# Two of the four last parts of the next item's token gather moved behind the scatter, in each expert item

## The chip, the cores and the metric

The kernel runs on one core of one Trainium2 chip. The metric is the device time of one launch in microseconds (us), lower is better. PE is TensorE's matmul, PEld its weight load, DVE VectorE, ACT ScalarE, SP the engine that starts the weight transfers. A matmul in float32 leaves two MATMUL and two LDWEIGHTS records in the trace, so a group of 4 matmuls reads x8.

## What is computed

Two decoder layers on 256 tokens of 1024 values, everything in float32. Each layer is a mixer (three attention patterns in one, a forgetting attention, an output projection), a layer norm, a mixture of 16 experts, and a second layer norm. The change lies in the expert part:

```python
def expert_block(args):
    xblk, e = args                      # tokens routed to expert e
    a = jax.nn.silu(xblk @ w_gate[e]) * (xblk @ w_up[e])
    return a @ w_down[e]                # three 1024 x 1024 float32 matrices each
...
out = jnp.zeros((T + 1, D)).at[row_tok].add(yb * row_gate[:, None])[:T]
...
h = layer_norm(DEEPNORM_ALPHA * h + y, ln2_g[l], ln2_b[l])
```

Every token goes to two experts of one group, and the two results are weighed by its gates.

## The kernel before

Both layers run as a hardware loop of two turns on every engine. In a layer the attention and the router come first. Then a second hardware loop (L874 on PE, its like on ACT and DVE) runs over the layer's **items**: an item is one expert with up to 32 tokens (tiny), 64 (narrow) or 128 (wide), and the kind of each item is worked out on the chip and read into registers. In the profiled execution there are 24 tiny, 9 narrow and 1 wide item in all, 16 or more per layer. The code of the three kinds lies in three branches, and those of tiny, narrow and wide items each have a part for experts of even and one for experts of odd number.

What an item does on PE, in program order:

- wait for `xg_ready` (the item's tokens, gathered and copied to SBUF as `xg`), then take the branch by kind and by odd or even;
- the gate and the up product (`quarter` L592 for tiny, `halves` L580 for narrow, `wide_product` L687 for wide), with weights that stream through `ring`;
- `gather` (L567) for the next item, parts 0 to 3. A gather is a matmul with a 0/1 matrix `place_t` made by DVE; part k brings 128 of the 1024 values of each token, so the eight parts fill two banks of `lo`, and the semaphore `gathered` counts up after part 3 and after part 7;
- the turning of the activations, then the down product into `lo`;
- gather, parts 4 to 7;
- the scatter (L645 in `scatter_halves`, L727 in the wide item), a matmul that adds the item's result `y` to the layer's sum in `acc`. It waits for `y_ready`.

DVE has its own fixed order for an item: `place_gates` (L1180) for this item and `place_tokens` (L1173) for the next, the product of gate and up, the copy of the turned gates, `copy_gathered(turn, 0)`, then the copy of the down product to `y` (L1390 tiny, L1399 narrow, L1409 wide; it ends in `y_ready`), then `copy_gathered(turn, 1)`. The latter (L1187) waits for `gathered` after part 7, copies the second bank to `xg` and raises `xg_ready`. After the last item DVE waits for `scattered` and starts the second layer norm (L1062). The last item of a layer gathers for an item that doesn't exist, and DVE copies that too.

SP streams each expert's gate, up and down matrices, 4 MB each in two transfers of 2 MB, into `ring`: gate and up have two homes (even and odd experts), down has one. In program order it waits for the gate of item e to be read (`gate_half`, `gate_done`), loads the gate of e + 2, does the same with up, then waits for down of e and loads down of e + 1 (L347).

The tail of an item before the change:

```python
pe.wait_ge(placeT_ready, g + 1)
gather(range(4, KB))
scatter_halves(g)
```

Of the kernel before, what the change touches and what calls it, by code (L numbers as in the profile page):

```python
# [43 lines left out]
KB = D // P  # L44
# [114 lines left out]
def build(nc, x, w_in, w_out, w_gate, w_up, w_down, small, router, ln, consts, out):  # L159
    with ExitStack() as ctx:  # L160
# [277 lines left out]
        def _(pe):  # L438
# [123 lines left out]
            def gather(ks, release=None):  # L562

                for k in ks:
                    for t in range(TB):
                        mm = nc.tensor.matmul(lo[:, 2 + k // 4, (k % 4) * P:(k % 4 + 1) * P],  # L567
                                              h[:, t, k * P:(k + 1) * P], place_t[:, t],
                                              start=(k % 4 == 0 and t == 0), stop=(t == 1), skip_group_check=True)
                        if release is not None and k == ks[0] and t == 0:  # L570
                            mm.then_inc(release, 1)
                    if k % 4 == 3:
                        mm.then_inc(gathered, 1)

            def halves(bank, lhsT, s, kk, start, stop):

                for half in range(2):
                    at = kk * D + half * 512
                    mm = nc.tensor.matmul(lo[half * W:(half + 1) * W, bank, :], lhsT, ring[:, s, at:at + 512],  # L580
                                          start=start, stop=stop, skip_group_check=True)
                return mm

            def turn_gates():

                for t in range(TB):
                    mm = nc.tensor.transpose(lo[:, 3, t * P:(t + 1) * P], place_tg[:, t], ident)
                mm.then_inc(placeT_done, 1)

            def quarter(at, bank, lhsT, s, col, start, stop):  # L590

                return nc.tensor.matmul(lo[at * T:(at + 1) * T, bank, :], lhsT, ring[:, s, col:col + 512],  # L592
                                        start=start, stop=stop, skip_group_check=True)
# [19 lines left out]
            def tiny_item(full, g, turn):  # L613

                pe.wait_ge(place_ready, turn + 1)
                gather(range(3))
                pe.wait_ge(act_ready, g + 1)
                turn_gates()
                for b in range(4):
                    mm = nc.tensor.transpose(lo[:, 1, b * W:(b + 1) * W], act[0:W, b * P:(b + 1) * P], ident[0:W, 0:W])  # L620
                mm.then_inc(act_turned, 1)
                gather(range(3, 4))
                pe.wait_ge(act_t_ready, g + 1)
                for s in range(4):
                    if s % AT_ONCE == 0:
                        pe.wait_ge(ring_full[DOWN + s], full)
                    for half in range(2):
                        for kk in range(2):
                            f = 2 * s + kk
                            at = (f % 4) * W + (f // 4) * T  # L630
                            mm = quarter(2 * half + kk, 0, act_t[:, at:at + T], DOWN + s, kk * D + half * 512,
                                         s == 0, s == 3)
                    if s % AT_ONCE:
                        mm.then_inc((down_half, down_done)[s // AT_ONCE], 1)
                pe.wait_ge(placeT_ready, g + 1)
                gather(range(4, KB))
                scatter_halves(g)

            def scatter_halves(g):

                pe.wait_ge(y_ready, g + 1)
                for t in range(TB):
                    for half in range(2):
                        r = slice(half * W, (half + 1) * W)
                        mm = nc.tensor.matmul(acc[:, 2 * t + half, :], place_gt[r, t * P:(t + 1) * P], y[r, 0:512],  # L645
                                              start=False, stop=True, skip_group_check=True)
                mm.then_inc(scattered, 1)
# [12 lines left out]
            def narrow_item(full, g, turn):  # L660

                pe.wait_ge(place_ready, turn + 1)
                gather(range(3))
                pe.wait_ge(act_ready, g + 1)
                for b in range(4):
                    mm = nc.tensor.transpose(lo[:, 1, b * P:(b + 1) * P], act[:, b * P:(b + 1) * P], ident)
                mm.then_inc(act_turned, 1)
                turn_gates()
                gather(range(3, 4))
                pe.wait_ge(act_t_ready, g + 1)  # L670
                for s in range(4):
                    if s % AT_ONCE == 0:
                        pe.wait_ge(ring_full[DOWN + s], full)
                    for kk in range(2):
                        f = 2 * s + kk
                        at = (f % 4) * P + (f // 4) * W
                        mm = halves(0, act_t[:, at:at + W], DOWN + s, kk, f == 0, f == KB - 1)
                    if s % AT_ONCE:
                        mm.then_inc((down_half, down_done)[s // AT_ONCE], 1)
                pe.wait_ge(placeT_ready, g + 1)  # L680
                gather(range(4, KB))
                scatter_halves(g)

            def wide_product(bank, lhsT, s, kk, start, stop):
                for half in range(2):
                    at = kk * D + half * 512
                    mm = nc.tensor.matmul(lo[:, bank + half, :], lhsT, ring[:, s, at:at + 512],  # L687
                                          start=start, stop=stop, skip_group_check=True)
                return mm
# [12 lines left out]
            def wide_item(full, g, turn):  # L702

                pe.wait_ge(act_ready, g + 1)
                for b in range(KB):
                    mm = nc.tensor.transpose(lo[:, b // 4, (b % 4) * P:(b % 4 + 1) * P], act[:, b * P:(b + 1) * P],
                                             ident)
                mm.then_inc(act_turned, 1)
                turn_gates()  # L710
                pe.wait_ge(place_ready, turn + 1)
                gather(range(4))
                pe.wait_ge(act_t_ready, g + 1)
                for s in range(4):
                    if s % AT_ONCE == 0:
                        pe.wait_ge(ring_full[DOWN + s], full)
                    for kk in range(2):
                        f = 2 * s + kk
                        mm = wide_product(0, act_t[:, f * P:(f + 1) * P], DOWN + s, kk, f == 0, f == KB - 1)
                    if s % AT_ONCE:  # L720
                        mm.then_inc((down_half, down_done)[s // AT_ONCE], 1)
                pe.wait_ge(placeT_ready, g + 1)
                gather(range(4, KB))
                pe.wait_ge(y_ready, g + 1)
                for t in range(TB):
                    for half in range(2):
                        mm = nc.tensor.matmul(acc[:, 2 * t + half, :], place_gt[:, t * P:(t + 1) * P],  # L727
                                              y[:, half * 512:(half + 1) * 512],
                                              start=False, stop=True, skip_group_check=True)
                mm.then_inc(scattered, 1)  # L730

            def turn_raw(t, banks, release=None):

                for b in range(2):
                    for i in range(4):
                        k = 4 * b + i
                        mm = nc.tensor.transpose(banks[b][:, i * P:(i + 1) * P], raw[:, t, k * P:(k + 1) * P], ident)
                        if release is not None and k == 0:
                            mm.then_inc(release, 1)
                    mm.then_inc(turned, 1)  # L740
# [45 lines left out]
            with pe.Fori(0, DEPTH) as l:  # L786
# [87 lines left out]
                with pe.Fori(0, n) as j:  # L874
# [10 lines left out]
                    with pe.If(kind < TINY_KINDS):  # L885
                        with pe.If(odd < 1):
                            tiny_gate_up(EVEN, UP, even_full, even_full)
                        with pe.Else():
                            tiny_gate_up(ODD, ODD_UP, odd_full, odd_up_full)
                        tiny_item(full, g, turn)  # L890
# [545 lines left out]
```

## Time and profile before

| | us |
|---|---|
| three runs | 1303.62, 1308.72, 1309.84 (median 1308.72) |
| the profiled execution | 1304.05 |
| its span, first to last instruction | 1302.4 |
| PE busy in it | 1094.1 (84%) |
| DVE busy | 351.2 (27%) |
| ACT busy | 184.8 (14%) |
| weights and the rest read from HBM | 443.11 MB, mean 341 GB/s over the span |

The profile cuts the span into 40 slices of 32.6 us. The expert items of the first layer run from about 174 to 613 us, those of the second from about 793 to 1289 us; the rest is attention and router. Busy shares are means over these stages, so each stage is read by itself, from the chain of waits, the DMA's share in short stretches, and the timeline around one item's end.

### The profile page before, as it was taken

How to read it: one execution, taken by the hardware profiler on the slowest of the kernel's cores; microseconds unless marked ns; L12 is line 12 of the kernel's file. 1: busy time of each engine (PE TensorE's matmuls, PEld its weight loads, DVE VectorE, ACT ScalarE, POOL GpSimd, SP SyncE). 2: the span in 40 equal slices, each digit the busy share in tenths (PEclk: the TensorE clock that was granted, in tenths of full speed). 3: DMA queues.
4: the chain of work that ended last, by engine and by line, in shares of the span. 5: the costliest groups of instructions: out<-in, count | busy, mean ns of one | idle time of the engine just before them, and what ended most of it. 6: DMA issues, size and time to landing. Idle time of an engine off the chain costs nothing.

```text
span 1302.4 us, 17517 instructions
## 1 busy us (share of the span) xinstructions
PE 1094.1 (84%) x6296; PEld 550.1 (42%) x6297; DVE 351.2 (27%) x853; ACT 184.8 (14%) x375; POOL 4.6 (0%) x12
## 2 busy tenths in 40 slices
PE   7999979799966779777999997898998876776585
PEld 5676543344422333323676653343443432232232
DVE  0764650011111111113366463111011111111123
ACT  2233310000010000010223321001001000010000
POOL 0000000000000000000000000000000000000000
PEclk9999998899987789889899998899999988787898
DMA  9914389999999999999931542359989999999994
GB/s 376 384 65 187 130 368 428 389 428 428 429 430 428 428 428 430 429 408 422 391 130 65 194 184 108 154 233 405 429 333 421 430 427 429 428 429 429 427 406 193
DMA packets 34712, 444.71 MB, mean 341 GB/s; under 512 B 4080, under 2 KB 4336, under 8 KB 5872
## 3 DMA queue, kind: packets, MB, share of 16 engines
q1 hardware_dynamic: 33520, 439.97, 80.9%
q0 software_dynamic: 1152, 4.19, 0.8%
q8 instruction: 26, 0.43, 0.1%
q14 instruction: 14, 0.11, 0.0%
HBM read 443.11 MB, written 1.05 MB: 341 GB/s over the span
## 4 chain that ended last, share of the span: by engine, by line
PE 55%; DMA 37%; issue 4%; DVE 3%; ACT 0%; DVEq 0%; ACTq 0%; SPq 0%
DMA ring<-in_w_down_dram 37%; PE lo L580 12%; PE acc L491 9%; PE lo L592 8%; PE acc L469 5%; PE lo L567 5%; PE lo L687 3%; PE acc L555 3%; PE acc L645 2%; PE lo L555 1%; PE acc L533 1%; PE lo L521 1%; PE lo L510 1%; PE acc L754 1%; PE lo L508 1%
## 5 line engine op out<-in xcount | busy, mean ns | idle before, releaser
L592 PE MATMUL lo<-ring,work 128*32 128x512 f32 x2304 | 297.5, 664 | 140.9 <-DMA ring<-in_w_down_dram 125.8
L592 PEld LDWEIGHTS lo<-ring,work 128*32 128x32 f32 x2304 | 78.3, 117 | 336.9 <-issue 172.5
L580 PE MATMUL lo<-ring,work 128*64 128x512 f32 x864 | 196.4, 611 | 28.4 <-issue 21.6
L567 PEld LDWEIGHTS lo<-work,h 128*128 128x128 f32 x1152 | 138.1, 193 | 64.2 <-issue 59.2
L567 PE MATMUL lo<-work,h 128*128 128x128 f32 x1152 | 156.8, 285 | 3.7 <-DVE work L1311 1.9
L580 PEld LDWEIGHTS lo<-ring,work 128*64 128x64 f32 x864 | 63.3, 141 | 154.1 <-issue 146.2
L491 PE MATMUL acc<-ring 128*128 128x256 f32 x512 | 119.2, 388 | 0.0
L491 PEld LDWEIGHTS acc<-ring 128*128 128x128 f32 x512 | 98.4, 195 | 20.0 <-issue 7.4
L1026 ACT ACTIVATE work<-lo 64x512 f32<-64x512 f32 x24 | 14.3, 594 | 488.2 <-PE lo L592 488.2
L1390 DVE COPY work<-lo 128x512 f32<-128x512 f32 x24 | 16.6, 692 | 231.2 <-PE lo L592 231.2
L469 PE MATMUL acc<-ring 128*128 128x512 f32 x128 | 62.5, 633 | 3.8 <-ACT ring L924 3.8
L645 PE MATMUL acc<-work 64*128 64x512 f32 x264 | 65.6, 615 | 0.0
L1187 DVE COPY work<-lo 128x512 f32<-128x512 f32 x68 | 47.0, 692 | 59.8 <-PE lo L567 59.6
L1385 DVE TENSOR_TENSOR work<-lo,work 64x512 f32<-64x512 f32 x24 | 16.4, 682 | 140.3 <-ACT work L1026 140.3
L687 PE MATMUL lo<-ring,work 128*128 128x512 f32 x96 | 41.6, 593 | 0.6 <-issue 0.6
L555 PE MATMUL acc<-ring,work 128*128 128x512 f32 x88 | 41.7, 603 | 0.0
L1394 DVE TENSOR_TENSOR work<-lo,work 128x512 f32<-128x512 f32 x9 | 6.2, 692 | 127.2 <-PE lo L580 127.2
L469 PEld LDWEIGHTS acc<-ring 128*128 128x128 f32 x128 | 24.6, 202 | 31.3 <-issue 30.0
L1180 DVE TENSOR_SCALAR work<-cst,rank_tab,gate_tab 128x128 f32 x68 | 20.5, 344 | 60.1 <-issue 60.1
L1137 DVE TENSOR_TENSOR work<-work,cst 32x512 f32<-32x512 f32 x48 | 32.8, 683 | 13.0 <-ACT work L937 11.5
L1026 ACT ACT_TABLE_LOAD x24 | 30.8, 1283 | 21.9 <-issue 21.9
L645 PEld LDWEIGHTS acc<-work 64*128 64x128 f32 x264 | 22.7, 186 | 19.5 <-issue 15.5
(190 smaller groups left out, 658.5 us busy)
## 6 DMA issues: line engine op xcount, KB each, us to landing
ring<-in_w_gate_dram SPq DMA_DIRECT2D x64, 2048.0 KB, 18.4
ring<-in_w_up_dram SPq DMA_DIRECT2D x64, 2048.0 KB, 24.2
ring<-in_w_down_dram SPq DMA_DIRECT2D x64, 2048.0 KB, 23.8
ring<-in_w_in_dram SPq DMA_DIRECT2D x24, 1024.0 KB, 26.2
ring<-in_w_out_dram SPq DMA_DIRECT2D x8, 1024.0 KB, 29.0
ln_gb<-in_ln_dram POOLq DMA_DIRECT2D x8, 512.0 KB, 11.4
cst<-in_consts_dram SPq DMA_DIRECT2D x1, 1420.0 KB, 17.5
h<-in_x_dram SPq DMA_DIRECT2D x1, 1024.0 KB, 5.2
```

The lines of the kernel that those rows point to most:

```text
L469: mm = nc.tensor.matmul(acc[:, 3 if u else 1, :], actT[:, k, t * P:(t + 1) * P], ring[:, s, (k % 4) * CH:(k % 4 + 1) * CH], start=(k == 0) ...
L491: mm = nc.tensor.matmul(acc[:, 1, i * SEQ:(i + 1) * SEQ], ring[:, s, at:at + P], actT[:, k, :], start=(k == 0 and i == 0), stop=(k == KB - ...
L555: mm = nc.tensor.matmul(banks[half], oT[:, k, t * P:(t + 1) * P], wout[:, k, half * 512:(half + 1) * 512], start=(k == first), stop=(k == ...
L567: mm = nc.tensor.matmul(lo[:, 2 + k // 4, (k % 4) * P:(k % 4 + 1) * P], h[:, t, k * P:(k + 1) * P], place_t[:, t], start=(k % 4 == 0 and t ...
L580: mm = nc.tensor.matmul(lo[half * W:(half + 1) * W, bank, :], lhsT, ring[:, s, at:at + 512], start=start, stop=stop, skip_group_check=True)
L592: return nc.tensor.matmul(lo[at * T:(at + 1) * T, bank, :], lhsT, ring[:, s, col:col + 512], start=start, stop=stop, skip_group_check=True)
L645: mm = nc.tensor.matmul(acc[:, 2 * t + half, :], place_gt[r, t * P:(t + 1) * P], y[r, 0:512], start=False, stop=True, skip_group_check=True)
L687: mm = nc.tensor.matmul(lo[:, bank + half, :], lhsT, ring[:, s, at:at + 512], start=start, stop=stop, skip_group_check=True)
L1026: nc.scalar.activation(silu[0:W, 0:512], lo[W:P, 0, :], ACT.Silu).then_inc(silu_done, 1)
L1137: nc.vector.tensor_tensor(turned_part[to], raw[at], sin[at], ALU.mult)
L1180: nc.vector.tensor_scalar(place_tg[:, t], places[:, bass.ds(kind * P, P)], rank_tab[:, t, bass.ds(expert, 1)], gate_tab[:, t, bass.ds(expe ...
L1187: op = nc.vector.tensor_copy(xg[:, 4 * half:4 * half + 4, :], lo[:, 2 + half, :].rearrange("p (k s) -> p k s", k=4))
```

## The change

In the three kinds of item the second half of the gather is cut in two: parts 4 and 5 stay ahead of the scatter, parts 6 and 7 are issued after it. No instruction is added or taken away, and neither DVE's, ACT's nor SP's program changes. The semaphore `gathered`, which counts up after part 7, so comes after the scatter. Line numbers behind the edits move by one to three.

```diff
@@ tiny_item (and narrow_item, word for word the same)
                 pe.wait_ge(placeT_ready, g + 1)
-                gather(range(4, KB))
+                gather(range(4, 6))
                 scatter_halves(g)
+                gather(range(6, KB))
@@ wide_item
                 pe.wait_ge(placeT_ready, g + 1)
-                gather(range(4, KB))
+                gather(range(4, 6))
                 pe.wait_ge(y_ready, g + 1)
                 for t in range(TB):
                     for half in range(2):
...
                 mm.then_inc(scattered, 1)
+                gather(range(6, KB))
```

PE, the end of a tiny item (L592 down product, L567 gather, L645 and then L646 scatter), before:

```order
L592 MATMUL lo<-ring,work 32x512 [waits ring_full10]
L592 MATMUL lo<-ring,work 32x512 x7
L567 MATMUL lo<-work,h 128x128 [waits placeT_ready]
L567 MATMUL lo<-work,h 128x128 x7
L645 MATMUL acc<-work 128x512 [waits y_ready]
L645 MATMUL acc<-work 128x512 x3
L885 UNCONDITIONAL_BRANCH
```

and with the change:

```order
L592 MATMUL lo<-ring,work 32x512 [waits ring_full10]
L592 MATMUL lo<-ring,work 32x512 x7
L567 MATMUL lo<-work,h 128x128 [waits placeT_ready]
L567 MATMUL lo<-work,h 128x128 x3
L646 MATMUL acc<-work 128x512 [waits y_ready]
L646 MATMUL acc<-work 128x512 x3
L567 MATMUL lo<-work,h 128x128 x4
L888 UNCONDITIONAL_BRANCH
```

Four of the eight gather matmuls (two parts of two matmuls each) went from ahead of the scatter to behind it; they are now the last work of the item on PE.

PE, the end of the wide item (L687, then L689, the down product; L727, then L729, the scatter), before:

```order
L687 MATMUL lo<-ring,work 128x512 x7
L567 MATMUL lo<-work,h 128x128 [waits placeT_ready]
L567 MATMUL lo<-work,h 128x128 x7
L727 MATMUL acc<-work 128x512 [waits y_ready]
L727 MATMUL acc<-work 128x512 x3
```

and with the change:

```order
L689 MATMUL lo<-ring,work 128x512 x7
L567 MATMUL lo<-work,h 128x128 [waits placeT_ready]
L567 MATMUL lo<-work,h 128x128 x3
L729 MATMUL acc<-work 128x512 [waits y_ready]
L729 MATMUL acc<-work 128x512 x3
L567 MATMUL lo<-work,h 128x128 x4
```

The same move, with a scatter of four full-height matmuls. DVE's order stays as it was. From the copy of `y` in a narrow item over the end of the loop to the second layer norm it reads, in the kernel before:

```order
L1399 COPY work<-lo 128x512 [waits down_done]
...
L1187 COPY work<-lo 128x512 [waits gathered]
L1392 UNCONDITIONAL_BRANCH
L1373 REGISTER_ALU
L1373 COMPARE_AND_BRANCH
L1412 REGISTER_ALU
L1062 BN_STATS stats<-acc 128x6 [waits scattered]
```

Nothing moved here: the copy that waits for `gathered` stands ahead of the layer norm that waits for `scattered`, before and after.

## Rows read from the trace of the kernel before

**Rows 1.** The page: the chain that ended last; GB/s in 40 slices.

```profile
PE 55%; DMA 37%; issue 4%; DVE 3%; ACT 0%; DVEq 0%; ACTq 0%; SPq 0%
GB/s 376 384 65 187 130 368 428 389 428 428 429 430 428 428 428 430 429 408 422 391 130 65 194 184 108 154 233 405 429 333 421 430 427 429 428 429 429 427 406 193
```

**Rows 2.** Stretches: us, busy PE, PEld, DVE, ACT, POOL; PEclk, DMA share, GB/s.

```profile
238.00:242.00 4.00, 4.00 (x22) 1.41 (x20) 0.00 (x0) 0.00 (x0) 0.00 (x0) 0.98 0.65 197
242.00:300.00 58.00, 56.95 (x296) 24.55 (x294) 8.56 (x18) 4.93 (x6) 0.00 (x0) 1.00 0.99 422
...
864.00:880.00 16.00, 15.52 (x100) 6.34 (x104) 3.16 (x7) 1.28 (x1) 0.00 (x0) 1.00 0.01 4
...
973.00:977.00 4.00, 4.00 (x42) 1.18 (x37) 0.00 (x0) 0.00 (x0) 0.00 (x0) 1.00 0.36 70
977.00:1240.00 263.00, 191.93 (x1328) 81.28 (x1324) 40.22 (x84) 22.72 (x30) 0.00 (x0) 0.87 1.00 428
```

**Rows 3.** Timeline of SP, the weight transfers: start us, us, engine, line, what.

```profile
240.59 3.69 SPq L347 DMA_DIRECT2D ring<-in_w_gate_dram  x2
...
268.76 3.69 SPq L347 DMA_DIRECT2D ring<-in_w_gate_dram  x2
...
296.79 3.69 SPq L347 DMA_DIRECT2D ring<-in_w_gate_dram  x2
...
879.35 3.69 SPq L347 DMA_DIRECT2D ring<-in_w_gate_dram  x2
...
975.28 3.69 SPq L347 DMA_DIRECT2D ring<-in_w_gate_dram  x2
```

**Rows 4.** Timeline, a tiny item's end and the next one's start.

```profile
1244.26 2.05 PE L567 MATMUL lo<-work,h 128*128 128x128 f32 x16
...
1244.40 0.69 DVE L1390 COPY work<-lo 128x512 f32<-128x512 f32 x1 [14.32 <-PE lo L592]
...
1246.25 1.99 PE L645 MATMUL acc<-work 64*128 64x512 f32 x8
1246.35 0.69 DVE L1187 COPY work<-lo 128x512 f32<-128x512 f32 x1 [1.26 <-PE lo L567]
...
1248.38 0.19 PEld L592 LDWEIGHTS lo<-ring,work 128*32 128x32 f32 x8 [0.97 <-issue]
1248.41 7.07 PE L592 MATMUL lo<-ring,work 128*32 128x512 f32 x64 [0.17 <-issue]
```

**Rows 5.** Timeline, the scatter between two narrow items.

```profile
290.57 1.99 PE L645 MATMUL acc<-work 64*128 64x512 f32 x8
...
292.88 13.96 PE L580 MATMUL lo<-ring,work 128*64 128x512 f32 x64 [0.32 <-issue]
```

**Rows 6.** Timeline, layer one's first item: the copy to xg, then the gate.

```profile
172.60 1.07 ACT L1016 COPY work<-lo 128x512 f32<-128x512 f32 x2 [10.60 <-PE lo L567]
...
174.36 0.19 PEld L592 LDWEIGHTS lo<-ring,work 128*32 128x32 f32 x8 [1.98 <-issue]
...
174.39 7.07 PE L592 MATMUL lo<-ring,work 128*32 128x512 f32 x64 [1.82 <-ACT work L1016]
```

**Rows 7.** Timeline, the end of the wide item and the tiny one behind it.

```profile
966.28 1.29 DVE L1409 COPY work<-lo 128x512 f32<-128x512 f32 x2 [13.04 <-PE lo L687]
...
967.86 3.60 PE L727 MATMUL acc<-work 128*128 128x512 f32 x8
...
971.39 0.16 PEld L592 LDWEIGHTS lo<-ring,work 128*32 128x32 f32 x8 [0.76 <-issue]
```

**Rows 8.** Timeline, the end of the second layer's items.

```profile
1287.17 0.69 DVE L1187 COPY work<-lo 128x512 f32<-128x512 f32 x1 [1.26 <-PE lo L567]
...
1289.10 1.29 DVE L1062 BATCH_NORM_STATS2 stats<-acc 128x6 f32<-128x512 f32 x2 [1.24 <-PE acc L645]
```

**Rows 9.** Timeline of PE, gate and up products behind longer gaps.

```profile
235.29 7.19 PE L580 MATMUL lo<-ring,work 128*64 128x512 f32 x26 [6.41 <-issue]
...
826.60 9.76 PE L592 MATMUL lo<-ring,work 128*32 128x512 f32 x64 [3.44 <-issue]
```

More of the change, by code:

```diff
@@ L722, in wide_item @@
                 pe.wait_ge(placeT_ready, g + 1)
-                gather(range(4, KB))
+                gather(range(4, 6))
                 pe.wait_ge(y_ready, g + 1)
@@ L730, in wide_item @@
                 mm.then_inc(scattered, 1)
+                gather(range(6, KB))
             def turn_raw(t, banks, release=None):
```

## The prediction

> **What bounds the kernel now.** I read the chain first. It is PE for 55% of the span and DMA for 37% [rows 1], so neither is the bound throughout, and the question is where each holds. The GB/s slices answer roughly: some 428 GB/s through most of both expert stages, far less at the start of the second one (108, 154, 233, then 333 once more, [rows 1]). Short stretches then say where the DMA runs dry. In the first layer it has a hole at 238 to 242 us and is full from there [rows 2]. In the second it stands still from 864 to 880, is low once more at 973 to 977, and is then full for 263 us at 428 GB/s [rows 2]. Each hole ends with SP issuing a gate transfer, at 240.59, 879.35 and 975.28 [rows 3]; SP had waited for PE to read the gate of an item. So up to such a point the time belongs to PE, and whatever makes PE later there moves the whole transfer stream behind it. Behind it, the stream sets the time, and a PE that is a microsecond later only waits a microsecond less for its next down matrix. The very end of each layer, after the last down half has landed, is PE's and DVE's again.
>
> The item's end is next. In a tiny one the second gather starts at 1244.26 and the scatter at 1246.25, while DVE copies y from 1244.40 to 1245.09 [rows 4]. y is therefore there 1.1 us before PE gets to the scatter. DVE then copies xg, 1246.35 to 1247.04, under the scatter, and the next gate's weights are loaded at 1248.38 [rows 4]. The scatter hides the copy completely. The gap behind it is 0.17 us here and 0.32 us in a narrow item [rows 4, 5].
>
> **What the change does at an item's end.** PE's work stays the same: 2.0 us of gather and 2.0 us of scatter. The gather ahead of the scatter shrinks to half, 1.0 us, against a copy of y that is ready 0.83 us after the gather's start (1245.09 less 1244.26). That wait stays hidden, with 0.2 us to spare; I allow 0.05 us for a later first weight load. So nothing is won: PE did not wait for y before. What is lost is the cover of the xg copy. `gathered` now comes with the last matmul of the item, about 1248.3. DVE starts 0.11 us after PE has finished the gather (as 1246.35 follows the gather's end at 1246.24), copies for 0.69, and is done near 1249.1. From there to the next gate's weight load I need a row in which PE waits at exactly that place: the first item of the layer. There the copies end at 172.60 + 1.07 = 173.67 and the weights load at 174.36, 0.69 us later [rows 6]; two branches lie in between. Sum: 1249.1 + 0.69 = 1249.8, against 1248.38. **An open boundary costs 1.4 us.** Its bounds: with nothing between copy and load it is 0.7; with the whole 1.34 us that lie between 1247.04 and 1248.38 it is 2.05.
>
> Which value holds turns on what the 1.34 us are. Either PE's sequencer was already waiting at `xg_ready` and the path from there really takes 1.34, or it came later, held up by reading two register values for the loop. I take 0.69, because in [rows 6] the wait for the copy is certainly the last. The page "TensorE: Matmul & The Clock Gate" of the Trainium skill (its table of specs) gives TensorE's queue a depth of 64, which would let the sequencer run past an item's 32 tail instructions and stand at the wait early; by that rule the boundary would cost 2.05 us and the total near 19. No row here shows the depth, and [rows 6] has the shorter path; the case is the first rival below.
>
> The wide item is different. Its copy of y takes two instructions and ends at 966.28 + 1.29 = 967.57, some 0.5 us later than a half gather from 966.08 or so would end, so PE waits for y and the scatter starts near 967.65 instead of 967.86. Its first gate load behind came at 971.39, with no gap [rows 7]. Now: scatter to 971.3, gather to 972.3, copy 972.4 to 973.1, gate at 973.8. **The wide boundary costs 2.4 us** (1.7 to 3.1).
>
> **Which boundaries count.** First layer: the hole closes at 240.59, when item 2 has read its first gate half; it began at 235.29 [rows 9]. Ahead of it lie the boundaries 0 to 1 and 1 to 2, both with the change's gap in full: 2 x 1.4 = 2.8. Behind it the DMA is full, but barely: a narrow item takes PE 296.79 - 268.76 = 28.0 us [rows 3], and its six transfers of 2.1 MB at 428 GB/s take 29.4. With 1.4 more PE needs 29.4 as well. The gate issue at 268.76 comes about 3 us before the six transfers from 240.59 are through (first data some 1.9 us after the issue, then 29.4), and with the same 1.9 us of latency the margin is 1.2 us. The boundary 2 to 3 eats 1.4 of it, and the next ones hold it level. I put **0.5** for this (0 to 1.5). Items behind 350 us are tiny, their PE work is a fraction of 29.4, and nothing of the change is seen.
>
> Second layer: 879.35 is the gate of item 3, behind the boundaries 0 to 1, 1 to 2 and 2 to 3. Boundary 3 to 4 is hidden, item 4 waits for its down matrix. Items 4 to 5 (into the wide one) and 5 to 6 (out of it) lead to 975.28. That is 4 x 1.4 + 2.4 = **8.0**. All boundaries behind 977 are hidden under the 263 us of full DMA [rows 2].
>
> **The two layer ends.** One could expect a gain of 1 us here, since the scatter ends a microsecond earlier. But DVE's copy of xg stands ahead of the layer norm in its program. Today that copy is done at 1287.86 and DVE idles 1.24 us until the scatter ends [rows 8]. Now the copy waits for part 7, behind the scatter. All PE work still ends at about 1289.05, just ahead of today's statistics, DVE copies 1289.16 to 1289.85, and the statistics follow at once, as DVE's instructions queue back to back: 1289.9 against 1289.10. **0.8 us each**, 1.6 in all, between 0.7 and 2.0 each (if leaving the loop on DVE took the 1.24 us that it now has free). The first layer's end reads alike, and the next layer's PE work waits for it.
>
> **Sum:** 2.8 + 0.5 + 8.0 + 1.6 = **12.9 us**. The profiled execution becomes 1304.05 + 12.9 = 1317.0. The three runs lie at 1303.6 and at 1308.7 to 1309.8, so I add to the middle, 1306.5, and say 1319.5.
>
> **Rivals.**
>
> *The longer path.* 1.34 us from xg to gate at every boundary: 6 x 2.05 + 3.1, and narrow items of 30.1 us against 29.4 of DMA, which cost 2 instead of 0.5; with 1.6 for the ends +19.0, or 1325.5. For it: the row of 1248.38. Against: [rows 6].
>
> *The clock falls in the new gaps.* Behind 3.44 us of idle the gate and up products of a tiny item took 9.76 us instead of 7.07, at a granted clock of half (1.2 GHz) at first [rows 4, 9]. The new gaps are near 1.5 us; the first item's gate came after 1.82 us of idle and still took 7.07 [rows 6]. If two or three of the seven boundaries pay 2.7 each, +6.5: about 1326.
>
> *Code loading swallows part of it.* Three of the seven boundaries have a stall that nothing in the profile explains, two of over 6 us and one of 3.44 (two of the three in [rows 9]), each at the first visit of a branch, so I take them for the loading of code. If that starts before the wait for xg, it runs beside it and three times 1.4 fall away: +8.7, 1315.
>
> *The other side: the clock comes back sooner.* Four gate phases start at half clock behind a stall (the two of [rows 9] among them) and lose up to 2.7 us each (9.76 less 7.07), 10.8 together at most, on the path that counts. Where the clock rises depends on when the work starts. If a start 1 to 3 us later cut all four to nothing, and the boundaries cost only 0.7 each, the sum would be 6 x 0.7 + 1.7 + 1.6 - 10.8 = -3.3, 1303. It decides from the point at which these phases run in 7.1 (tiny) and 14.0 us (narrow) right away. Nothing in the trace speaks for it except that the loss is there to be regained.
>
> **How the numbers follow.** Forecast 0.62, longer path 0.13, clock falls 0.10, code loading 0.10, clock back sooner 0.05. The range takes in the first four: low 1303.6 + (6 x 0.7 + 1.7 + 2 x 0.7) = 1311 by the lower bounds, high 1309.8 + 19.4 = 1329, rounded up by half a microsecond. A difference of under 0.5%, 6.5 us, can't be told from none. The forecast is twice that. Of the forecast's own 0.62 I give 0.03 to ending under 6.5, of the code loading case 0.05 more, of the last rival 0.02 to a gain and 0.03 to none: slower 0.87, same 0.11, faster 0.02.
>
> **What would show it.** In the profile after: y copied before PE gets to the scatter in tiny and narrow items, and a wait of 0.5 us for y in the wide one; PE idle 1.5 us ahead of each gate product, put down to DVE's copy L1190, which starts 0.1 us behind part 7; the SP issue of 240.59 near 243.4, that of 879.35 some 8 later (3.3 of the first layer, 0.8 of its end, 4.2), that of 975.28 some 12 later; the full stream of 263 us as long as before; the first statistics of a layer right behind an xg copy. It is wrong if the gaps stay near 0.3 us, if the DMA shows no hole where I count PE, or if the statistics start ahead of the xg copy.

## The result and the profile after

The change makes the kernel slower by 0.95% (ratio 1.0095, 95% interval 1.0078 to 1.0112), or about 12.4 us (10.2 to 14.6). The median is 1318.32 us against 1304.14 us, 7 runs each, so the medians lie 14.2 us apart; the 12.4 us are the ratio's. 1319.5 had been forecast. The profiled execution of the changed kernel took 1320.83 us, at a span of 1319.1, so it lies at the slow end of its own runs (1314.41 to 1321.48).

| | before, us | after, us |
|---|---|---|
| median | 1304.14 | 1318.32 |
| span of the profiled execution | 1302.4 | 1319.1 |
| PE busy | 1094.1 | 1105.9 |
| DVE busy | 351.2 | 351.0 |

Both kernels issue 17517 instructions. PE's busy time grew by 11.8 us with the same matmuls: 11.0 of it are the gather's (156.8 to 167.8), mostly because two halves of a gather read 1.16 us each in these records, and a whole one 2.05. The page of the changed kernel, the chain and GB/s in 40 slices (as [rows 1]):

```profile
PE 59%; DMA 32%; issue 5%; DVE 4%; DVEq 0%; ACT 0%; ACTq 0%; SPq 0%
GB/s 377 374 65 192 152 372 426 360 403 427 426 427 429 429 429 428 429 408 422 338 128 84 172 237 52 212 171 409 427 309 401 427 428 428 429 428 429 429 399 176
```

PE's share of the chain rose from 55 to 59% and the DMA's fell from 37 to 32%: the stretch in which the stream of weights sets the time starts later, it isn't slower (the rows from 992 us on, below). The groups of waits say what PE and DVE now wait for (who waited for whom: us, times, longest):

```profile
DVE work L1190 <- PE lo L567: 134.5, 59, 4.7
...
PE lo L592 <- DVE work L1190: 32.1, 21, 1.6
```

In the kernel before, DVE waited 59.6 us for the gather, and PE had no wait of this kind on DVE among its large ones. Now 21 gate products of tiny items wait for DVE's copy to xg, 1.5 us each. That is the new wait. A boundary is the end of one item and the start of the next. Here is one in full, between the same two tiny items as in [rows 4]. Timeline of the changed kernel, with start, duration, engine, line, tile, and in brackets the idle time before:

```profile
1262.29 1.99 PE L646 MATMUL acc<-work 64*128 64x512 f32 x8
...
1264.20 1.16 PE L567 MATMUL lo<-work,h 128*128 128x128 f32 x8
1265.40 0.69 DVE L1190 COPY work<-lo 128x512 f32<-128x512 f32 x1 [3.83 <-PE lo L567]
1266.76 0.19 PEld L592 LDWEIGHTS lo<-ring,work 128*32 128x32 f32 x8 [1.59 <-issue]
1266.79 1.49 PE L592 MATMUL lo<-ring,work 128*32 128x512 f32 x12 [1.43 <-DVE work L1190]
```

The scatter now comes first, then parts 6 and 7. DVE starts its copy when they are done and ends at 1266.09; PE loads the next gate's weights at 1266.76, 0.67 us later. Nothing of PE's work covers this: it idles for 1.43 us, where it had idled for 0.17.

The trace also holds the records of PE's sequencer, the part that reads the program and feeds the array, and they say where the 1.34 us between copy and gate went in [rows 4]. There the sequencer leaves the item's branch at 1245.17, loads its two register values from 1246.19 on (TENSOR_LOAD, 0.3 us each) and comes to the wait for `xg_ready` at 1247.64, 0.6 us after the copy's end at 1247.04. In the changed kernel it is there at 1264.84 and stands until 1266.13, just behind the copy's end. The same holds at every boundary without a long stall, in two traces of each kernel: before, the sequencer comes 0.5 to 1.2 us after the copy; with the change it comes 1.2 to 1.4 us ahead of the copy's end, 3.0 behind the wide item.

To see which of the 34 boundaries count, I cut both kernels at the same events. Each number is the time between two rows of a timeline; both kernels were profiled a second time, unedited (below), so there are two looks at each. "Issue of item n" is the first SP gate transfer behind the start of that item's gate product, and item 0 is a layer's first.

| stretch | before | after | forecast |
|---|---|---|---|
| start to item 0's second gather | 188.24, 189.44 | 187.97, 188.66 | 0 |
| to the issue of item 2 (240.59 in [rows 3]) | 52.35, 52.08 | 54.44, 54.82 | +2.8 |
| to the last item's second gather | 368.59, 369.20 | 371.16, 370.99 | +0.5 |
| to the statistics | 4.02, 4.02 | 4.81, 4.81 | +0.8 |
| to layer 2, item 0's second gather | 205.99, 206.26 | 206.89, 207.31 | 0 |
| to the issue of item 3 | 60.16, 60.24 | 65.09, 65.04 | +4.2 |
| to the issue of item 6 | 95.93, 95.94 | 99.52, 99.55 | +3.8 |
| to the last item's second gather | 309.80, 309.71 | 311.21, 309.58 | 0 |
| to the statistics | 4.02, 4.02 | 4.81, 4.81 | +0.8 |

The map holds where it can be tested. In the eighth row lie eleven boundaries, each with its 1.5 us gap, and the stretch reads 309.6 and 311.2 us; the kernels of the experiments read 309.7 to 309.8 or 311.0 to 311.7 there, and late_before, with the gather's order untouched, 311.2. So the change costs nothing in it. The sixth and seventh rows hold six boundaries and gain 8.5.

Two looks don't carry the first layer's rows. The two kernels of the experiments that keep the gather's order and the time (late_before, act_late_before) read 54.1 and 54.3 us in the second row and 370.9 and 370.7 in the third, as much as the changed kernel or nearly so. Of the 2.4 us that the second row gained, 1.2 are its two boundaries; the rest is two products behind long stalls, which run at half clock at first in every trace and together took 33.2 us on the mean in place of 31.9. In the fifth row, where I forecast nothing, the two looks gain 1.0, and all fourteen traces spread over 204.2 to 208.1.

The DMA's holes and the full stretch behind them, in the changed kernel (columns as in [rows 2]):

```profile
864.00:890.00 26.00, 24.27 (x148) 10.72 (x148) 4.28 (x9) 2.47 (x3) 0.00 (x0) 1.00 0.26 109
...
988.00:992.00 4.00, 4.00 (x40) 1.42 (x36) 0.48 (x2) 0.00 (x0) 0.00 (x0) 1.00 0.35 74
992.00:1256.00 264.00, 195.94 (x1328) 82.46 (x1320) 40.23 (x84) 22.72 (x30) 0.00 (x0) 0.88 1.00 428
```

From 992 the stream runs full for 264 us at 428 GB/s, as it did from 977.

### The profile page after: what moved, and what is told of

It is laid out like the page before. It is cut to its first block, busy times and chain, and to the rows that moved or that the text cites. A ratio compares the mean times of both kernels' runs of the same rounds, so it can differ in the third digit from the quotient of the medians.

```text
span 1319.1 us, 17517 instructions
## 1 busy us (share of the span) xinstructions
PE 1105.9 (84%) x6296; PEld 556.0 (42%) x6297; DVE 351.0 (27%) x853; ACT 184.8 (14%) x375; POOL 4.6 (0%) x12
## 4 chain that ended last, share of the span: by engine, by line
PE 59%; DMA 32%; issue 5%; DVE 4%; DVEq 0%; ACT 0%; ACTq 0%; SPq 0%
DMA ring<-in_w_down_dram 32%; PE lo L580 15%; PE lo L592 9%; PE acc L491 9%; PE lo L567 6%; PE acc L469 5%; PE lo L689 3%; PE acc L555 3%; PE acc L646 2%; PE lo L555 1%; PE acc L533 1%; PE lo L521 1%; DVE work L1190 1%; PE lo L510 1%; PE acc L757 1%
## 5 line engine op out<-in xcount | busy, mean ns | idle before, releaser
L592 PE MATMUL lo<-ring,work 128*32 128x512 f32 x2304 | 296.6, 662 | 141.4 <-DMA ring<-in_w_down_dram 101.6
L580 PE MATMUL lo<-ring,work 128*64 128x512 f32 x864 | 200.5, 622 | 30.9 <-issue 26.5
L592 PEld LDWEIGHTS lo<-ring,work 128*32 128x32 f32 x2304 | 78.4, 117 | 317.7 <-issue 185.9
L567 PEld LDWEIGHTS lo<-work,h 128*128 128x128 f32 x1152 | 142.8, 195 | 92.8 <-issue 87.8
L567 PE MATMUL lo<-work,h 128*128 128x128 f32 x1152 | 167.8, 291 | 3.0 <-DVE work L1314 1.9
L646 PE MATMUL acc<-work 64*128 64x512 f32 x264 | 65.6, 615 | 0.0
L1388 DVE TENSOR_TENSOR work<-lo,work 64x512 f32<-64x512 f32 x24 | 16.4, 683 | 116.2 <-ACT work L1029 116.2
L689 PE MATMUL lo<-ring,work 128*128 128x512 f32 x96 | 41.6, 593 | 1.9 <-issue 1.9
L469 PEld LDWEIGHTS acc<-ring 128*128 128x128 f32 x128 | 24.9, 203 | 31.9 <-issue 30.6
L1140 DVE TENSOR_TENSOR work<-work,cst 32x512 f32<-32x512 f32 x48 | 32.8, 683 | 12.4 <-ACT work L940 11.0
L646 PEld LDWEIGHTS acc<-work 64*128 64x128 f32 x264 | 22.7, 186 | 19.6 <-issue 15.8
## 6 DMA issues: line engine op xcount, KB each, us to landing
ring<-in_w_gate_dram SPq DMA_DIRECT2D x64, 2048.0 KB, 17.5
```

The lines of the kernel that those rows point to most:

```text
L469: mm = nc.tensor.matmul(acc[:, 3 if u else 1, :], actT[:, k, t * P:(t + 1) * P], ring[:, s, (k % 4) * CH:(k % 4 + 1) * CH], start=(k == 0) ...
L1140: nc.vector.tensor_tensor(turned_part[to], raw[at], sin[at], ALU.mult)
```

## The experiments

All kernels were timed against the kernel before on the same chips; a ratio is followed by its 95% interval.

### Is it the copy to xg, and does it matter how much is moved?

One part behind the scatter in place of two:

```diff
-                gather(range(4, 6))
+                gather(range(4, 7))
...
-                gather(range(6, KB))
+                gather(range(7, KB))
```

> Only part 7 of the gather stands behind the scatter, parts 4 to 6 ahead. Theory (the cost of a boundary is the copy to xg that no PE work covers any more, plus the 0.7 us from there to the next gate): it doesn't matter how many parts stand behind, as long as the last one does. Gaps of 1.4 to 1.8 us ahead of the gate as with the change, statistics at a layer's end right behind the copy, and the time of the changed kernel, +0.9 to +1.1% over before (about +12 us). Rival (the cost grows with what is moved, such as each switch between scatter and gather matmuls): half of it, about +6 us, gaps near 0.9 us.

Measured: 1.0098 (1.0074 to 1.0122), +12.8 us. The time from an item's second gather to the next gate is the same as with two parts behind to 0.1 us: 5.75 against 5.75 us at the second narrow-to-narrow boundary, 5.64 against 5.64 at a tiny one, 4.81 at both layer ends. Only behind the wide item it is shorter, 7.16 against 7.60, because three parts ahead of the scatter hide y's copy but for 0.04 us. Half the move costs the whole price. What counts is that the last part, and with it `gathered`, stands behind the scatter.

All four parts behind the scatter:

```diff
-                gather(range(4, 6))
                 scatter_halves(g)
-                gather(range(6, KB))
+                gather(range(4, KB))
```

> All four parts stand behind the scatter, none ahead. Theory: the cover of DVE's copy of y is gone too. The y copy is ready some 0.9 us behind the last down matmul, so PE idles about 0.9 us ahead of each scatter (1.5 in the wide item) and again 1.5 us ahead of the gate. A boundary costs 2.4 us in place of 1.5, a layer's end 1.7 in place of 0.8, and a narrow item takes PE about 30.4 us against 29.3 of DMA. Sum near +21 us, +1.6% over before. Rival (the wait for y is hidden in the queue, only the copy to xg counts): as with the change, +12 us.

Measured: 1.0212 (1.0191 to 1.0234), +27.7 us, more than the 21 expected. The two waits stand in the trace one behind the other. Timeline of four_parts, a narrow item's end:

```profile
297.20 0.69 DVE L1399 COPY work<-lo 128x512 f32<-128x512 f32 x1 [6.54 <-PE lo L580]
298.01 0.33 PEld L645 LDWEIGHTS acc<-work 64*128 64x128 f32 x4 [1.73 <-issue]
298.04 1.99 PE L645 MATMUL acc<-work 64*128 64x512 f32 x8 [0.88 <-DVE work L1399]
...
299.96 2.05 PE L567 MATMUL lo<-work,h 128*128 128x128 f32 x16
302.05 0.69 DVE L1187 COPY work<-lo 128x512 f32<-128x512 f32 x1 [4.15 <-PE lo L567]
303.59 0.20 PEld L580 LDWEIGHTS lo<-ring,work 128*64 128x64 f32 x4 [1.77 <-issue]
303.59 1.94 PE L580 MATMUL lo<-ring,work 128*64 128x512 f32 x8 [1.58 <-DVE work L1187]
```

PE idles 0.88 us for y ahead of the scatter, as forecast, and 1.58 us for xg ahead of the gate. So the two parts that the change leaves ahead of the scatter are what hides y. Where the other 7 us are: the narrow items now follow each other at 30.4 us against 29.4 of transfers, and the stretch from item 2's issue to the layer's last gather grew to 373.4 us, as it did in one_part and only_narrow; the one from item 3's to item 6's issue grew by 8.3, where the expected prices make 5.7 (2.4 for a boundary, and 2.4 + 0.9 for the wide one). I didn't take it further apart, so this part stays open.

### Give the copy its cover back

PE waits for xg's second bank only where the gate product first reads it, at part 4; the first bank gets a semaphore of its own. The same edit on the changed kernel (late_after) and on the kernel before (late_before):

```diff
@@ narrow_matrix, gate only (and tiny_gate_up, wide_matrix)
                     if i % AT_ONCE == 0:
                         pe.wait_ge(ring_full[first + i], full)
+                    if i == 2 and turn is not None:
+                        pe.wait_ge(xg_ready, turn)
@@ the loop over the items
-                    pe.wait_ge(xg_ready, turn)
+                    pe.wait_ge(xg_half, turn)
@@ copy_gathered (and ACT's copies for a layer's first item)
-                if half == 1:
-                    op.then_inc(xg_ready, 1)
+                op.then_inc(xg_ready if half else xg_half, 1)
```

> The changed kernel, but PE waits for xg's second bank only ahead of part 4 of the gate product; the first bank has a semaphore of its own. The gather stays cut in two. Theory (uncovered copy): the first half of the gate covers the copy, the gaps fall from 1.4 to 1.8 us to under 0.5, the SP issues that end the DMA's holes move back by their share, and only the two layer ends still cost 0.8 each: +1 to +3 us over before (+0.1 to +0.2%). Rival (the later gather or the clock costs, not the wait): still +8 us or more.

> The kernel before with the same late wait for xg's second bank. If PE's sequencer already stood at the wait for xg in the kernel before (the longer path of 1.34 us from copy to gate), the gate now starts earlier and the gaps of 0.17 to 0.46 us vanish: up to -2 us. If it came later, held by the loop's register reads, nothing moves: 0 us, within 0.2%.

Measured: late_after 1.0055 (1.0035 to 1.0074), +7.2 us; late_before 0.9999 (0.9982 to 1.0015). Timeline of late_after at the second narrow-to-narrow boundary (its lines are a few numbers further on):

```profile
296.74 1.16 PE L568 MATMUL lo<-work,h 128*128 128x128 f32 x8
297.94 0.69 DVE L1197 COPY work<-lo 128x512 f32<-128x512 f32 x1 [3.40 <-PE lo L568]
298.26 0.20 PEld L581 LDWEIGHTS lo<-ring,work 128*64 128x64 f32 x4 [0.55 <-issue]
298.27 1.08 PE L581 MATMUL lo<-ring,work 128*64 128x512 f32 x4 [0.36 <-issue]
```

The gate starts 0.3 us after the copy has started, under it. The gap is 0.36 us, and from second gather to gate it is 4.53 us, against 4.29 before and 5.75 with the change. So 1.2 of the 1.46 us are the uncovered copy and its path; the other 0.24 stay, for the extra switch from gather to scatter and back (PE's own work from second gather to last matmul reads 4.16 us in place of 3.97). The gaps are gone, but the time isn't all back. 1.6 us of the 7.2 are the two layer ends (4.81, unchanged). 0.24 us at six boundaries, and 0.8 at the wide one, are 2.2. The 3.4 that are left I can't place; the interval of this run is 2.5 us to either side. late_after missed its forecast by some 4 us.

late_before answers a question that the prediction had left open. Had PE's sequencer stood at the wait for xg, moving that wait would have let the gate start earlier. It does not: 4.29 us at the same boundary, to 0.01. Timeline of late_before there:

```profile
289.90 2.05 PE L568 MATMUL lo<-work,h 128*128 128x128 f32 x16
...
294.19 1.08 PE L581 MATMUL lo<-ring,work 128*64 128x512 f32 x4 [0.32 <-issue]
```

In the kernel before, the sequencer came to the wait later than the copy, as its records said above.

### Take the copy out of the layer norm's way

ACT makes the second copy, behind its copy of the turned activations. DVE then waits for the gather before it overwrites `place_t` and before it writes `h`.

```diff
@@ ACT, the end of the loop's body
+                    a.wait_ge(gathered, a.snap(2 * start + 2 * l + 2 * j + 4))
+                    nc.scalar.copy(xg[:, 4:8, :], lo[:, 3, :].rearrange(
+                        "p (k s) -> p k s", k=4)).then_inc(xg_ready, 1)
@@ DVE
+                    v.wait_ge(gathered, turn * 2)
                     place_tokens(v.value_load(expert_i[...
...
-                        copy_gathered(turn, 1)
...
-                for t in range(TB):
-                    layer_norm(l, 1, t, acc_tok[:, t, :])
+                norm_stats(l, 1, 0, acc_tok[:, 0, :])
+                v.wait_ge(gathered, v.snap(2 * turn0 + 2 * n))
+                norm_apply(l, 1, 0, acc_tok[:, 0, :])
+                layer_norm(l, 1, 1, acc_tok[:, 1, :])
```

> The changed kernel, but the copy of the gather's second bank to xg is made by ACT, behind its copy of the turned activations, instead of by DVE; DVE waits for the gather before it overwrites place_t and before it writes h at a layer's end. Theory: at a layer's end the statistics no longer stand behind the copy, they start right behind the scatter, 1.8 us earlier than with the change and 1.0 earlier than before, so 3.6 us come back; the gaps ahead of the gate stay at 1.3 to 1.8 us (ACT's copy is about 0.15 us shorter). Sum +8 us over before (+0.6%). Rival (DVE's copy at the layer's end isn't on the path): no change against the changed kernel, +12 us.

> ACT makes the second copy and PE waits for it only ahead of part 4 of the gate product; gather cut in two as in the change. late_after was at +7.2 us, of which the two layer ends should be 1.6. With them turned from +0.8 to -1.0 each, 3.6 us come back: +3.5 us over before (+0.3%). If the 7.2 us came from the two ends in some larger way, it falls to 0 or below. If the ends don't count: +7 us.

> Both edits (copy by ACT, late wait) on the order of before, all of the gather ahead of the scatter. Theory: everything was hidden already, so 0 us within 0.2%. It is the reference for act_late_after: the difference of the two is the cost of cutting the gather when neither copy is in the way, by the traces so far 0.23 us per boundary on six boundaries, 0.8 at the wide one, less 1.0 at each layer end, so near 0.

Measured: act_after 1.0076 (1.0057 to 1.0094), +9.9 us; act_late_after 1.0016 (1.0005 to 1.0027), +2.1; act_late_before 0.9996 (0.9982 to 1.0009). First the layer's end with the change itself, then with ACT's copy (act_after):

```profile
1304.10 1.16 PE L567 MATMUL lo<-work,h 128*128 128x128 f32 x8
...
1305.29 0.69 DVE L1190 COPY work<-lo 128x512 f32<-128x512 f32 x1 [3.37 <-PE lo L567]
1305.90 1.29 DVE L1065 BATCH_NORM_STATS2 stats<-acc 128x6 f32<-128x512 f32 x2
```

```profile
1296.84 1.16 PE L567 MATMUL lo<-work,h 128*128 128x128 f32 x8
1296.96 1.30 DVE L1067 BATCH_NORM_STATS2 stats<-acc 128x6 f32<-128x512 f32 x2 [2.29 <-PE acc L646]
1298.04 0.58 ACT L1048 COPY work<-lo 128x512 f32<-128x512 f32 x1 [9.29 <-PE lo L567]
```

With the change DVE waits for a gather that nobody needs, copies it, and only then starts the statistics; with the copy on ACT it starts them 0.1 us behind the scatter. From the last second gather to the statistics it is 4.02 us before, 4.81 with the change, and 3.12 with ACT's copy. Two layer ends give 3.4 us, and the runs have 2.5 (9.9 against 12.4) and 5.1 (2.1 against 7.2), each of them known to about 3 us only. With both edits the cut gather costs 2.1 us against before, and against its own reference act_late_before the same 0.2%: with the copy hidden at the boundaries and out of the layer norm's way the cut is nearly free, and nowhere a gain. No version of it beats the kernel before.

### Which kinds of item carry it

The change in one kind of item alone, the other two as before. The narrow and the wide one:

```diff
@@ only the named kind (tiny_item, narrow_item or wide_item)
-                gather(range(4, KB))
+                gather(range(4, 6))
                 scatter_halves(g)
+                gather(range(6, KB))
```

> The change in tiny items alone. Theory (a boundary counts only where PE sets when the DMA's hole ends): in the first layer only 0 to 1 counts (code stall, 0.55), in the second 1 to 2 and 4 to 5 at 1.5 each, and both layer ends at 0.8, since the last items are tiny: +5 us (+0.4%), though 24 of 34 items are changed. Rival (every boundary counts a little): 24 of 34, +9 us.

> The change in narrow items alone (9 of 34). Theory: boundaries on the path are 1 to 2 in the first layer (0.7 behind a code stall) and the drain of the DMA's margin in the narrow run behind it (about 1), 0 to 1 (0.3, code stall) and 2 to 3 (1.45) in the second, plus 1.7 for each gate product that then starts at half clock; no layer end, the last items are tiny. +3.5 to +5 us. With tiny alone at +8.7 and wide at +2.3 the three should add to the change's 12.4 within the error. Rival (each boundary counts alike): 9 x 0.36 = +3.3, so this run alone doesn't part them; its trace does: the layer ends stay at 4.02 us from the second gather to the statistics, and the stretch between the second layer's issues of items 3 and 6 stays near 95 us.

> The change in the one wide item. Theory: 5.31 us from its second gather to the next gate become 7.2 to 7.6, and as its boundary leads to the transfer that ends the DMA's last hole, the whole kernel is +2.0 to +2.3 us later (+0.17%). Rival (each boundary counts alike, 12.4 / 34): +0.4 us. Everything else in the trace as before.

Measured: tiny 1.0067 (1.0041 to 1.0094), +8.7 us; narrow 1.0038 (1.0019 to 1.0058), +5.0; wide 1.0029 (1.0014 to 1.0043), +3.8. One wide item of 34 carries 0.14% (1.8 us) at the lower end of its interval, far over the +0.4 us that an equal share would be; that rival falls. Its boundary, in only_wide:

```profile
966.65 1.05 PE L567 MATMUL lo<-work,h 128*128 128x128 f32 x8
968.19 3.70 PE L727 MATMUL acc<-work 128*128 128x512 f32 x8 [0.49 <-DVE work L1410]
971.73 1.05 PE L567 MATMUL lo<-work,h 128*128 128x128 f32 x8
974.25 6.21 PE L592 MATMUL lo<-ring,work 128*32 128x512 f32 x56 [1.47 <-DVE work L1188]
```

PE waits 0.49 us for y, then 1.47 for xg. From second gather to gate it is 7.60 us, against 5.31 in [rows 7]: 2.3 us, which is what was forecast for the whole kernel; the 3.8 measured hold it within their interval (1.8 to 5.6). Tiny items cost more than my count of 5, and that run can't be told from "each boundary a little" (9). The stretches of its trace can: the layer ends read 4.81, item 3's to item 6's issue 98.96 (before 95.93; 1.7 of it is the wide item's gate and up product, which started at half clock), and the first warm boundary of the second layer has its gap, while the one behind the narrow item has none. The three alone add to 17.5 us, with a joint error of about 5; whether they truly overlap when put together isn't settled.

### Second looks

> The changed kernel unedited, a second look. The gaps of 5.6 to 5.9 us from second gather to next gate repeat to 0.1 us; which gate products run at half clock (15.58 us in place of 13.88) does not. Layer ends 4.81 us, the stretch from the issue of item 6 to the last item's end 309.7 to 311.7 us.

> The kernel before unedited, a second look. Gaps 4.1 to 4.6 us and layer ends 4.02 us repeat; the stretch up to the first layer's issue of item 2 and the one behind it vary by up to 2 us with the clock, so the span lies 0 to 5 us above that of the first profile.

Single runs: 1320.54 and 1305.85 us. The gaps repeat to 0.1 us where neither code loading nor the clock has a part, and so do the layer ends. The two looks at before agree, but their first layer isn't typical of its order, as late_before and act_late_before showed above; this is why the profiled spans differ by some 16 us and the timed runs by 12.4.

## Why the prediction was right

**No gain at y.** Confirmed. PE didn't wait for y before; with the change it doesn't in tiny and narrow items, and waits 0.49 us in the wide one (0.5 forecast). four_parts shows the wait of 0.88 us that the two remaining parts hide.

**1.4 us per open boundary.** Measured in the changed kernel, from second gather to next gate: 5.75 against 4.29, 5.93 against 4.44, 5.63 against 4.15, so 1.46 to 1.49 us. A few grew by more, such as the one shown in full (6.04 against 4.14), whose first gather half took 1.6 us at a granted clock of 0.68. The path from copy to gate, taken as 0.69 us from [rows 6], measured 0.67 at the boundary above. The longer-path rival (2.05) falls by this row, by late_before, and by the sequencer's records: it came 0.6 us after the copy, held by y's copy and then by the register values, the second of the prediction's two readings. Of the 1.46, 0.24 is the extra switch between gather and scatter, which I had at 0.05. The Trainium skill ("TensorE: Matmul & The Clock Gate", table of specs) gives TensorE's queue a depth of 64, which had put the sequencer at the wait early in my rival. In this loop the wait isn't reached that early; how deep the queue is no run here shows.

**The wide boundary 2.4.** Measured 2.29 in both the changed kernel (7.60 against 5.31) and only_wide.

**Which boundaries count.** Behind the last hole nothing, as forecast. Ahead of it 8.5 us in the second layer, against 8.0, and this agreement is partly luck. The sixth row has the clock in it (below). In the seventh the boundary into the wide item grew by 2.4 and 2.5 us where I had 1.4, as its gather ran at a granted clock of 0.64; in exchange the wide item's turning and first gather, which in both looks at before ran slowly (granted clock 0.63, 2.84 us for the 16 gather records), ran at full clock (1.95 us), and the item became 1.65 us shorter. The first layer's rows can't confirm their part: 2.8 forecast, 1.2 found at its two boundaries.

**Code loading: the step that was off.** I gave the three boundaries with a stall 1.4 each and the case that a stall swallows it 0.10. They grew from 10.17 to 10.72, from 10.38 to 11.08 and from 7.41 to 7.72 us (second looks: 10.09 to 10.97, 10.46 to 10.67, 7.46 to 7.54), 0.1 to 0.9 and on the mean 0.5. So most of the 1.4 is swallowed. The three together grew by 1.4 us, where I had 4.2. Kernels that leave these boundaries alone spread nearly as far, from 10.1 to 10.7, from 10.0 to 10.6 and from 7.4 to 7.7 us.

The prediction took the stalls for the loading of code, and the kept traces bear it out. In all fourteen of them each of the three stalls holds one branch record of PE's sequencer, at the end of an item, that takes 3.3 to 6.7 us. Of the 164 branches in the traces of before and after only two more are as long, behind the first layer's last item and ahead of the second layer's first; all others take at most 0.5. Inside each of the long ones starts a packet of the DMA queue that the page lists as `q8 instruction`, of 16 KB (two packets in some traces of the first stall). The branch of the second stall, before: from 225.79 for 6.22 us, the packet at 229.48. With the change: from 225.96 for 6.67, the packet at 230.10. The branch stands ahead of the wait for xg. With the change DVE's copy is done 4.5, 5.2 and 2.1 us before the sequencer comes to that wait at the three boundaries (second look: 4.8, 4.9 and 1.9). So the wait costs nothing there, and the rival's mechanism was right: the loading covers the copy as the scatter did.

**The clock: the step that made up for it.** I gave it 0.10 that new gaps drop the clock, at 2.7 us each. In the two traces of the changed kernel 3 gate products of narrow items behind a gap of 1.72 to 1.77 us (gate and up together) took 15.65 us in place of 13.95, or 1.7 more. One, item 2 of the second layer, did so in both looks. The granted clock around it, in the changed kernel and then before (the same product):

```profile
855.20:858.00 2.80, 2.72 (x8) 0.97 (x10) 0.86 (x4) 0.00 (x0) 0.00 (x0) 0.56 1.00 427
858.00:861.50 3.50, 3.50 (x16) 1.15 (x14) 0.23 (x2) 0.00 (x0) 0.00 (x0) 0.86 0.98 421
861.50:870.00 8.50, 8.50 (x42) 2.93 (x40) 0.00 (x0) 0.60 (x1) 0.00 (x0) 1.00 1.01 432
```

```profile
847.30:850.00 2.70, 2.61 (x12) 0.95 (x14) 1.08 (x4) 0.00 (x0) 0.00 (x0) 1.00 1.01 431
850.00:853.50 3.50, 3.50 (x20) 1.24 (x18) 0.00 (x0) 0.00 (x0) 0.00 (x0) 1.00 1.00 431
```

PEclk is 0.56 at first, so mostly the lower level (1.2 of 2.4 GHz), and full after some 3 us. That is why the sixth stretch grew by 4.9: 0.3 (the stalled boundary; 0.1 in the second look) + 1.5 + 1.45 + 1.7. The other of the three lies in the first layer in one of the two looks. Its third stretch grew by some 2.2 us in both, where I had 0.5, and that part stays open.

**The clock comes back sooner.** The rival of 0.05 didn't come true in the changed kernel: the products behind the stalls took 16.4 to 16.8 us in the first layer and 9.8 to 9.9 in the second. It isn't empty, though. In late_before, late_after and only_tiny the second layer's product ran at full clock from its start (7.07 us) behind 3.6 to 3.8 us of idle, and the sixth stretch was 1.0 to 2.5 us shorter than before.

**The layer ends.** 0.79 measured, 0.8 forecast, at each of the two ends in both looks, and act_after shows the mechanism by turning it into -0.90.

**Sum.** Forecast 12.9; in the runs 12.4. The stretches of the four looks add to some 16, since both profiled executions of the changed kernel were 2 us slower than its median. The total is right partly by luck: two misses, code loading (-2.8) and the clock (+1.7 and more), have opposite signs, and I had given each the rank of a rival at 0.10. The price of an open boundary, of the wide one and of the layer ends was right in its mechanism.

## What to carry to other kernels

Before moving work from one side of a step to the other, ask what it covers on each side, and look at who waits for its last instruction: here the moved half carried the semaphore that starts a copy on another engine, and that copy's cover was the step it was moved behind. A wait that is already hidden can't be made cheaper; the move cost 1.5 us at each open boundary, whether one or two parts went, and more with all four. And a delay has a price only up to the last point where PE still decides when the transfer queue runs dry: 1.5 us at each of eleven boundaries behind it cost nothing. Where something else already holds the engine, here three stalls of the sequencer, the same wait is free too.

## What the runs showed of the hardware

The clock falls in shorter gaps than I had expected. In six traces of kernels whose gaps at boundaries without a long stall stay under 0.7 us (before twice, late_before, late_after, act_late_before, act_late_after) no gate product behind such a boundary ran at half clock; a layer's last item, which waited 1.4 to 2.8 us for its weights, did in some. In eight traces with gaps of 1.3 to 1.9 us nine did. All nine stood behind gaps of 1.72 to 1.9 us, had a granted clock of 0.52 to 0.62 over their first 2.8 us and were 1.7 us longer (gate and up together 15.65 for 13.95 us in narrow items, 29.43 for 27.73 in the wide one). Seventeen others behind gaps of the same length ran at full clock (granted 1.00), so behind such a gap 9 of 26 products started slowly. Tiny items' products behind gaps of 1.3 to 1.65 us took 7.07 us throughout, save where they waited for their weights.

Reading two register values at the head of an item takes the sequencer 1.4 us (1246.19 to 1247.60), which is why it came to the wait later than a copy that was done under the scatter.

A copy moved off the engine that made it doesn't help where it was hidden: 0.69 us on DVE and 0.58 on ACT for 128 x 512 values, and no difference to the whole (act_late_before, 0.9996).
